# Meta tokens' 16x16 triangular system solved by forward substitution on VectorE, and the mix's small products padded to 128

## The reference

```
decay = exp(where(causal, g[:, None] - g[None, :], -inf))
a_mat = where(strict, (k_beta @ k.T) * decay, 0)
sol = triangular_solve(a_mat + eye, [v * beta, k_beta * exp(g)], lower=True, unit_diagonal=True)
w_val, w_key = sol[:, :DV], sol[:, DV:]
v_new = w_val - w_key @ S
o = q_dec @ S + qk_intra @ v_new
S = S * g_last + k_dec.T @ v_new
```

## Time and profile before

| | us |
|---|---|
| median of 3 runs | 2951.88 |
| lowest and highest | 2951.57, 2952.71 |
| span of the profiled execution | 2950.3 |
| one head of the mix: mix_row issued at 554.04 and at 613.36 | 59.3 |
| start to start of big products of 272 columns (603.34, 603.46, 603.59, 603.71, 603.84, 603.96, 604.09) | 0.125 |
| from 550 to 700: PE busy 150.00 of 150, DVE 104.56, ACT 80.88, granted clock 1.00, DMA share 0.41 | |

### The profile page before, as it was taken

One profiled execution on the slowest core, in us unless ns is written; L12 is line 12 of the kernel. 1 busy time (PEld: TensorE's weight loads), 2 busy tenths in 40 slices (PEclk: granted clock), 3 DMA queues, 4 the chain that ended last, 5 costly groups with the idle time before them and its releaser, 6 DMA issues.

```text
span 2950.3 us, 52683 instructions
## 1 busy us (share of the span) xinstructions
PE 2896.8 (98%) x18731; PEld 2578.3 (87%) x18731; DVE 1996.8 (68%) x3460; ACT 1430.8 (48%) x2496; POOL 277.1 (9%) x229
## 2 busy tenths in 40 slices
PE   7999999999999899999999999999999999999998
PEld 6999999999999788887888888888888888888877
DVE  6667776777676556666775665656777666777865
ACT  5555655565556344444444443534545545445542
POOL 0000000000000000002540000000450002400014
PEclk9999999999999899999999999999999999999999
DMA  5434343434344355556555555565655444544444
GB/s 192 145 121 140 122 147 121 136 127 143 125 133 129 102 184 188 188 185 199 181 186 191 183 188 184 185 193 179 197 179 164 150 158 150 185 151 143 133 132 171
DMA packets 128957, 472.88 MB, mean 160 GB/s; under 512 B 14368, under 2 KB 14368, under 8 KB 128672
## 3 DMA queue, kind: packets, MB, share of 16 engines
q1 hardware_dynamic: 126144, 459.46, 48.1%
q0 software_dynamic: 2656, 11.33, 1.2%
HBM read 468.50 MB, written 2.24 MB: 160 GB/s over the span
## 4 chain that ended last, share of the span: by engine, by line
PE 94%; issue 2%; POOL 2%; DVE 1%; ACT 1%; DMA 1%; POOLq 0%; DVEq 0%; ACTq 0%
PE bank L287 35%; PE bank L288 17%; PE bank L289 10%; PE bank L290 9%; PE bank L291 9%; PE bank L729 1%; PE bank L801 1%; PE bank L780 1%; PE bank L964 1%; PE bank L797 1%; POOL late_sum L436 1%; POOL late_sq L432 1%; PE bank L958 1%; PE bank L1036 1%; PE bank L1035 1%
## 5 line engine op out<-in xcount | busy, mean ns | idle before, releaser
L263 DVE TENSOR_TENSOR w_lo<-raw,w_hi 128x1024 fp32r<-128x1024 f32 x866 | 1063.4, 1254 | 186.5 <-ACT w_hi L257 176.2
L257 ACT ACTIVATE w_hi<-raw 128x1024 fp32r<-128x1024 f32 x866 | 898.1, 1052 | 467.8 <-PE bank L288 452.5
L287 PE MATMUL bank<-u,w_hi 128*128 128x512 f32 x2288 | 820.2, 400 | 3.2 <-DVE ya L1831 3.2
L289 PE MATMUL bank<-u,w_hi 128*128 128x272 f32 (+2 forms) x2064 | 640.2, 310 | 9.2 <-DVE w_lo L263 7.2
L288 PE MATMUL bank<-u,w_lo 128*128 128x256 f32 x2288 | 644.8, 282 | 0.0
L287 PE MATMUL bank<-ya,w_hi 128*128 128x512 f32 x1792 | 633.1, 398 | 0.0
L290 PE MATMUL bank<-u,w_hi 128*128 128x272 f32 (+2 forms) x2064 | 589.7, 286 | 0.0
L291 PE MATMUL bank<-u,w_lo 128*128 128x272 f32 (+2 forms) x2064 | 589.4, 286 | 0.0
L287 PEld LDWEIGHTS bank<-u,w_hi 128*128 128x128 f32 x2288 | 431.3, 188 | 104.8 <-issue 9.4
L288 PE MATMUL bank<-ya,w_lo 128*128 128x256 f32 x1792 | 502.4, 280 | 0.0
L288 PEld LDWEIGHTS bank<-u,w_lo 128*128 128x128 f32 x2288 | 433.4, 189 | 0.4
(11 more groups left out here) (366 smaller groups left out, 3337.2 us busy)
## 6 DMA issues: line engine op xcount, KB each, us to landing
raw<-in_stream SPq DMA_DIRECT2D x868, 512.0 KB, 3.4
mix_row<-rows POOLq DMA_DIRECT2D x16, 408.0 KB, 4.0
xT<-in_xT SPq DMA_DIRECT2D x4, 544.0 KB, 6.0
h<-in_xT POOLq DMA_DIRECT2D x1, 2048.0 KB, 9.7
out_dram<-h SPq DMA_DIRECT2D x4, 512.0 KB, 2.6
consts<-in_consts POOLq DMA_DIRECT2D x1, 1921.0 KB, 9.4
vecs<-in_vecs POOLq DMA_DIRECT2D x1, 166.5 KB, 6.5
consts<-in_consts POOLq DMA_DIRECT2D x1, 137.0 KB, 5.8
```

The costliest lines, as they stand in the source:

```text
L257: act.activation(w_hi[:, slot], raw[:, slot], ACT.Copy).then_inc(hi_ready, 1)
L263: dve.tensor_tensor(w_lo[:, slot], raw[:, slot], w_hi[:, slot].bitcast(F32), ALU.subtract).then_inc(lo_ready, 1)
L287: pe.matmul(o, a, x, start=first, stop=False)
L289: pe.matmul(o, a, x[:, 0], start=first, stop=False)
```

## The change

It does four things in the mix.

1. The meta system leaves the doubling. b_mat is still made with its 144 columns; masks, levels and the constants cross and keep are 128 columns wide, and every 16x16 companion on PE is gone. In its place DVE solves the system itself: for all 128 columns of v at once (v is held transposed, a partition per column), sixteen small instructions in the tile solve_m, called "meta" 0, 1 and 2 in DVE_PLAN. The right side is v transposed times beta; then step j takes from the columns behind j the coefficient row j times column j.
2. The coefficients must stand on every partition for that. POOL writes the 16x16 corner of b_mat to DRAM (meta_rows) and reads it back to all 128 partitions (coef_m), two DMAs a head that follow one another. Its loop is unrolled, and the next head's mix_row is issued behind them; "row free" now comes from DVE after the first instruction of meta 0.
3. "meta v" is a transpose of solve_m to 16 rows. v_beta_m, its copy on ACT and the transpose of the meta part of v are gone.
4. The remaining small products get full size: kk's meta part is 128 rows and 128 weight columns with 16 moving ones; k_dec_m, v_new_m, f_pt_m and f_v_m have 128 rows, of which 112 are zeroed once at the start, so that meta state and fox out's first product contract over 128; step 6 uses 128 weight columns with 64 moving ones. "transpose" becomes a real transpose of one pass.

Some semaphores are merged or renumbered with it.

```diff
+        coef_m, solve_m = mt("coef_m", [P, META, META]), mt("solve_m", [P, META])
-        v_new_m = mt("v_new_m", [META, P])
+        v_new_m = mt("v_new_m", [P, P])
...
-            (86, "b mat"), (90, "unit q"), (92, "qk"), (94, "q dec"), (96, "level", 0), (98, "mask", 1),
-            (110, "unit fq"), (111, "level", 1), (111, "unit fk"), (113, "mask", 2), (114, "logits"),
+            (86, "b mat"), (90, "unit q"), (92, "qk"), (94, "q dec"), (96, "level", 0), (98, "mask", 1), (104, "meta", 0), (108, "meta", 1),
+            (110, "unit fq"), (111, "level", 1), (111, "unit fk"), (113, "mask", 2), (114, "meta", 2), (114, "logits"),
...
+            def meta_coefficients(n):
+
+                gp.wait_ge(sem("b mat"), 4 * n - 3)
+                gp.dma_start(meta_rows, b_mat[0:META, 0:META]).then_inc(sem("meta coef"), 16)
+                gp.wait_ge(sem("meta coef"), 32 * n - 16)
+                if n > 1:
+                    gp.wait_ge(sem("meta step"), META * (n - 1))
+                gp.dma_start(coef_m[:].rearrange("p j i -> p (j i)"), meta_rows.rearrange("j i -> (j i)")
+                             .partition_broadcast(P)).then_inc(sem("meta coef"), 16)
+
+            head_rows(1)
+            for n in range(1, HEADS + 1):
+                meta_coefficients(n)
+                if n < HEADS:
+                    head_rows(n + 1)
+                gp.wait_ge(sem("meta coef"), 32 * n)
...
-                for t0, w in MAIN_FIRST:
-                    mm = pe.matmul(bank[5][0:w, t0:t0 + w], kT[:, t0:t0 + w], kT[:, t0:t0 + w], start=True,
-                                   stop=True)
-                mm.then_inc(sem("kk"), 1)
+                for t0, w in MAIN:
+                    pe.matmul(bank[5][0:w, t0:t0 + w], kT[:, t0:t0 + w], kT[:, t0:t0 + w], start=True, stop=True)
+                pe.matmul(bank[5][:, 0:META], kT[:, 0:P], kT[:, 0:META], start=True,
+                          stop=True).then_inc(sem("kk"), 1)
...
             def pe_transpose(n):
                 pe.wait_ge(sem("inverse"), 16 * n - 15)
-                for t0, w in FOLDED:
-                    mm = pe.matmul(bank[5][0:w, t0:t0 + w], inv[0:w, 0, t0:t0 + w],
-                                   const("identity", t0, t0 + w, w), start=True, stop=True)
-                mm.then_inc(sem("prod sum"), 1)
+                pe.transpose(bank[5][:, main], inv[:, 0, main], ident).then_inc(sem("prod sum"), 1)
...
-                for t0, w in level_spans(lv):
-                    mm = pe.matmul(bank[5][0:w, t0:t0 + w], b_mat[0:w, t0:t0 + w], part[0:w, 1, t0:t0 + w],
-                                   start=True, stop=True)
-                mm.then_inc(sem("prod sum"), 1)
+                pe.matmul(bank[5][:, main], b_mat[:, main], part[:, 1, main], start=True,
+                          stop=True).then_inc(sem("prod sum"), 1)
...
+                to = slice(META + P // 2, FOLD) if LEVELS[lv] == LEVELS[-1] else main
+                pe.matmul(bank[6][:, to], part[:, 0, main], prod[:, to], start=True,
+                          stop=True).then_inc(sem("step"), 1)
+                pe.matmul(bank[7][:, to], prod[:, main], part[:, 0, to], start=True,
+                          stop=True).then_inc(sem("step t"), 1)
...
             def pe_meta_v(n):
-                pe.wait_ge(sem("inverse"), 16 * n - 8)
-                pe.wait_ge(sem("v beta"), 3 * n)
+                pe.wait_ge(sem("meta step"), META * n)
+                pe.wait_ge(sem("v beta"), 2 * n)
                 pe.wait_ge(sem("yb lo"), n)
-                pe.matmul(bank[3][:, 0:P], inv[0:META, 0, 0:P], v_beta_m[:, :], start=True,
-                          stop=True).then_inc(sem("v new m sum"), 1)
+                pe.transpose(bank[3][0:META, 0:P], solve_m[:, :], ident).then_inc(sem("v new m sum"), 1)
...
+            for x in (k_dec_m, v_new_m, f_pt_m, f_v_m):
+                dve.memset(x[:], 0.0).then_inc(sem("cleared"), 1)
...
+            def dve_meta(n, part_):
+                if part_ == 0:
+                    dve.wait_ge(sem("silu"), 4 * n - 3)
+                    if n > 1:
+                        dve.wait_ge(sem("v new m sum"), n - 1)
+                    dve.scalar_tensor_tensor(out=solve_m[:], in0=vT[:, 0:META], scalar=0.5, in1=row[:, 0, 0:META],
+                                             op0=ALU.mult, op1=ALU.mult).then_inc(sem("meta step"), 1)
...
+                    dve.sem_inc(sem("row free"), 1)
+                    dve.wait_ge(sem("meta coef"), 32 * n)
+                for j in range(5 * part_, 5 * part_ + 5):
+                    dve.wait_ge(sem("meta step"), META * (n - 1) + 1 + j)
+                    dve.scalar_tensor_tensor(out=solve_m[:, j + 1:], in0=coef_m[:, j, j + 1:],
+                                             scalar=solve_m[:, j:j + 1], in1=solve_m[:, j + 1:], op0=ALU.mult,
+                                             op1=ALU.subtract, reverse1=True).then_inc(sem("meta step"), 1)
```

132 lines of the change are left out of this document (57 added, 75 removed).

## The result

The changed kernel takes 2957.01 us (median of 20 runs, 2951.33 to 2962.60) against 2951.74 (20 runs, 2948.39 to 2957.46) of the one before: ratio 1.0015 [1.0009, 1.0022]. That is 5.3 us slower: small, but clear of the noise, and inside 0.2%, so "same" by the bound of the prediction. Forecast were 2926 and faster; the time lies outside the range of 2898 to 2952. The profiled execution is one of the longer ones, with a span of 2960.7 us.

The account below looks back on a forecast made before the run. PE bounds the mix, with DVE's new steps stalling it: -0.73 +0.40 +0.31 -0.18 -1.48 = -1.68 us a head, -26.8 for sixteen, plus 0.5 for memsets, from 2951.9 to 2926 us; range 2898 to 2952.

Parts of the forecast that it names:

- What bounds, and PE's gain: PE in the mix, busy 98%: small products at one full size save 5.23 us a head, 84 us if PE were alone.
- kk: PE before qk: the 16x16 pair becomes 16 moving columns under full weights, costing 0.16 instead of 0.33, saved 0.17.
- step 6: PE behind prod 4: four passes of 64 columns with full weights, taken as 0.35, saved 0.22.
- So 0.20 a step: DVE's small dependent steps: 0.15 each from a 128x3 row plus 0.04 between; batches of 1.07, 0.87 and 0.87 us.
- An instruction that waits for its predecessor starts some 0.04 after its end: DVE: gap assumed between dependent instructions, part of the 0.20 us a step.
- Prod 2: Second product with b_mat, counted from qk: 0.40 us a head later, PE stalling about 1.4 for DVE's batches 0 and 1.
- Prod 2 to prod 3: Stretch on PE: 6.00 becomes 6.31 us, 0.31 later, a stall of 1.3, through batch 2 between mask 2 and logits.
- Prod 3 to prod 4, and behind prod 4: PE: first stretch 0.18 us a head earlier with a stall of 0.8; behind it PE keeps its savings of 1.48.
- POOL's transfers: Coefficients to DRAM and back before batch 0: 6.3 us against 6.65 available, in time by 0.35.
- rival 2: Coefficients late at DVE: each microsecond beyond 6.65 costs 16; at 8.8, +0.5 a head, 2960 us; chance 0.11.
- steps of 0.30 (+1.3 a head): Rival on DVE: slower steps, 2947 us, or coefficients 1.3 to 2 late; within 0.2%; chance 0.09.
- One head for all: Mix: the head beginning at 602.41, some 59 us, stands for all; thirteen of fourteen others within 0.05 us.

Follow-up runs that it names:

- E3: Changed kernel without the 15 steps on DVE, transfers and padded products kept: 2898.4 us, ratio 0.9817.
- E5: Kernel before with the padding alone: every small product over 128 rows and columns, 16x16 system kept in the doubling, no steps, no transfers: 2915.0 us, ratio 0.9879.
- E1: Changed kernel with each of the 15 steps multiplying by the number 0.5 instead of a column of solve_m: 2940.1 us, ratio 0.9955.
- E12: Changed kernel with four of six waits and the raised count moved from before the first step to the second batch: 2952.3 us, ratio 1.0007.
- E7: Changed kernel with the second b_mat product (prod 2) moved from slot 111 to 116 in PE's order: 2939.5 us, ratio 0.9959.
- E2: Changed kernel with the coefficients transferred for head 1 alone and reused by heads 2 to 16: 2949.3 us, ratio 0.9991.
- E11: Changed kernel with the substitution on POOL, and prods 2 to 5, steps 3 and 4 and turn p later in PE's order: 2882.5 us, ratio 0.9767.
- E4: Changed kernel with the substitution on POOL, two instructions per step, the factor 0.5 in ACT's copy: 2892.9 us, ratio 0.9801.
- E13: Kernel before with the solve's first instruction and 15 steps added on DVE, result unused, no padding, no transfers: 2985.7 us, ratio 1.0117.

## Why the prediction was wrong, by its own steps

- **What bounds, and PE's gain:** right. 5.08 us a head against 5.23, and with the steps out of the way it shows (E3, E5). Two terms were off by 0.15 in sum: kk saved 0.12 (0.17) and step 6 0.12 (0.22). The Trainium skill's rule (TensorE: Matmul & The Clock Gate, LDWEIGHTS), weighed and set aside there, would have given 0.11 and 0.12; the trace agrees with it: a pass of 16 or 64 moving columns under full weights costs 0.11, the same as one of 128.
- **"So 0.20 a step":** the first step that failed. The row it came from had a number as its scalar; a column costs 0.06 more (E1), as two groups of the trace of before show (485 and 418 ns), and the steps start 0.26 apart. Worth 17 us in E1, the clock's share included.
- **"An instruction that waits for its predecessor starts some 0.04 after its end":** right for the steps and wrong ahead of the first one, where six waits and a raised count stand behind a short instruction: 0.36. Worth 0.25 us in an undisturbed head (E12), 2 to 5 us in all.
- **Prod 2, "+0.40"; measured +1.23.** These two make 0.99, a little more than the 0.83 that was missing; the mechanism, that nothing is hidden, was right.
- **Prod 2 to prod 3, "+0.31"; measured +0.62 at full clock, +1.25 in nine heads.** The path was right (ACT's copy of fv, which waits for PE), and because the forecast counts this stretch from prod 2, the later beginning of that path is in it: mask 2 comes 3.42 behind prod 2 (633.26-629.84), 3.66 before. The 0.31 missing at full clock is the step's price once more, 0.28 between mask 2 and logits; mask 2 is 0.24 earlier where I had 0.33. The other 0.63 is the clock. What the forecast didn't see is that the later beginning can be taken back: giving PE work at that place brings prod 3 1.13 nearer to prod 2 (E7).
- **The clock:** not in the prediction at all. The kernel before has no stretch of half clock in the mix, so its rows gave no price; but a forecast with a stall of 1.4 us in it, where there had been none, should have bounded what the engine does after one.
- **Prod 3 to prod 4, and behind prod 4:** -0.13 and -1.34 against -0.18 and -1.48, right.
- **POOL's transfers:** in time by 0.35 in the forecast. The writes of 1 KB landed in 2.3 to 4.6 us (median 2.6; 2.1 assumed), the reads in a median of 3.4, as taken. Late in some heads, 5 us by the waits and 8 by E2: rival 2's mechanism at 0.3 to 0.5 us a head, where it put 2.2.
- **Rivals:** none was it. Nearest is 3, "steps of 0.30 (+1.3 a head)", on the right engine: it would make a head 0.38 shorter, and head 10 is 0.30 shorter. Its +1.3 is what the steps (0.35 + 0.32 + 0.28 = 0.95 for the three batches) and the gap (0.32) come to. The clock and the late coefficients, 0.83 a head, come on top; together that is 2.10 of the 2.18 by which +0.50 a head misses -1.68. I gave DVE's chain one unknown, the step's price, and let the others stand at their nearest rows; the two that went against me there, scalar and gap, lie on the same bare chain and add up.
- **One head for all, "the same distances within 0.05 us":** that holds up to prod 6. Behind it heads 2 and 11 of the kernel before are 0.3 us longer than head 10, so the mean is 59.21 and not 59.16. This moves nothing in the forecast; the sum behind the result needs it.

## What to carry to other kernels

Where two engines take turns on one chain, a stall that a change creates moves the beginning of the next link as well: count the next term from the delayed instruction, and give the in-order engine something to do at that place (E7, E11). Take the work that must be dependent and small to an engine that nobody waits for, though it be three times slower there (E4), or leave it out of the change: padding to one shape alone was worth 37 us (E5). And price an instruction from a row with the same kinds of operands, not only of the same size.

## What the runs showed of the hardware that I had not expected

- A SCALAR_TENSOR_TENSOR on VectorE with a column of 128 values as its scalar takes 60 ns more than with a number in the instruction, at 1 to 15 columns (226 and 166 ns).
- Four waits that are long met, one more on the instruction ahead and a raised count cost 0.25 us behind a short instruction (a gap of 0.36 with them, 0.11 without, E12); where the instruction ahead is all that is waited for, the gap is 0.04.
- A TensorE stall of 2.06 us was followed by half the clock for 3.4 us in five of nine heads of the changed kernel and in seven of fifteen of E2, and by full clock in the others. Stalls of 1.1 us (E3, E13) and the eight of 1.45 us in E1 never were; those of 1.82 us in E7 were in two of fourteen heads. The clock costs 0.63 us a time here, where 3.4 us at half clock do 1.7 us of work: part of the slow stretch takes the place of the stall before prod 3.
- On GpSimd, tensor_scalar with a column takes 433 ns in the mean at 1 to 15 columns (single ones over 1 us) and tensor_tensor 286. VectorE's own instructions beside it were at most 9 ns longer.
